# Two transformer blocks on one core: decay rows in one tile, decay chains in steps, another order of the projections

## Chip, cores and metric
One core of a Trainium2 chip. The metric is the device time of one execution in microseconds (us), the median of several.

## What is computed
The reference runs two blocks over 512 tokens of width 1024, in float32. Block 1: a gated feed-forward part (inner width 2816), a mixer, a second feed-forward part. Block 2: a mixer, then a feed-forward part with a convolution. What the change touches lies in the mixers.

In the first mixer a state-space branch with 32 heads (four groups of eight) works in chunks of 128 tokens:

```python
dt = softplus(dt_raw + dt_bias)
a = (dt * a_head)                       # 32 heads x 512 tokens
a_cum = cumsum(a, within chunks)
Lmat = exp(where(causal, a_cum[l] - a_cum[s], -inf))
y_diag = (C B^T * Lmat) X
states = scan over chunks of B^T (exp(a_last - a_cum) X)
y_off = C prev * exp(a_cum)
```

Beside it runs a differential attention with 8 heads; both are gated and merged. In the second mixer a gated delta rule (8 heads in four pairs, chunks of 64 tokens) needs a similar decay row per head, `-exp(a_log) * softplus(..)`, summed up within chunks, and a row `beta` per head. Beside it an indexer scores all keys for each query, keeps the 128 highest, and a sparse attention uses only these.

## The kernel before
Everything is held transposed: features on the 128 partitions, the 512 tokens as columns. A projection (`ugemm`) makes a 128 x 512 tile from eight 128 x 128 blocks of a weight panel. Each float32 operand is split into a high part, rounded to fp32r, and the low rest; a block is three fp32r matmuls, high x high, high x low and low x high (L1679 to L1681), 24 a projection. A panel of 512 KB is loaded by SyncE, its high part is copied out by ScalarE (L2020) and its low part made by VectorE (L2321).

The order of all work is written by a planner when the kernel is built. It keeps an estimated clock for each engine, advanced by a table of costs, and draws steps from a main stream (the projections, in the order of the strings ORDER1 and ORDER2) and side streams (the recurrent parts, the attention, the indexer). A side step is issued once what it needs is due on TensorE's clock (`ready`), provided that VectorE's and ScalarE's clocks are at most AHEAD = 6.0 us in front of TensorE's. If no side can go, the main stream takes a quarter of a projection. Every engine then runs its own queue in the planned order, with semaphores. Tiles of 128 x 512 for intermediate values are pages of a pool (`fp`); `room(n)` holds the main stream until n pages are free.

In the order strings, of the first mixer: t is the projection of dt, z, g the projections of a group (z four, g six), b the branch output of a group (eight), a and c a head's q, k and v, E and F gates, r a wait for pages. Of the second: n the narrow panel with decay and beta, p a pair's six projections, x the indexer's inputs (all made ahead at the stage's start), z a pair's gates, h a hold until the pair's preparation (`gdn_prep`) is done, d a query head, k keys and values.

The parts that the change touches:

- `decay` (VectorE L2478 to L2490, ScalarE L2125 to L2129): one step that holds the softplus (L2456 to L2475), in which VectorE and ScalarE answer each other three times, the scan (L2486), the high part of the sums (L2129, rows 0 to 31 of page 16 of `mR`) and the low part (L2489, page 17).
- `ssd_front` (L1762 to L1768): for each of the 32 heads, the head's row of sums is spread over 128 partitions by two matmuls with a column of a 32-row identity as weights, one on the high and one on the low rows. `ssd_from` (L1770 to L1778) does so for two heads at once with `selR`, 16 times, and goes on with three 128 x 128 products (L1778). `ssd_y` (L1781 to L1787) multiplies 128 x 64 weights.
- `narrow` (VectorE L2651 to L2674): bias, sigmoid on ScalarE, copy (L2661), the same softplus over 128 rows, the scan, in one step. `gdn_decay` (L1839) and `gdn_att` (L1846) spread the decay and the beta row of two heads with 32-row weights of 64 columns; L1853 is the product behind L1846.
- `ix_score` and `ix_top` (L2839 to L2862): scores of the indexer, then 15 rounds for each of three query blocks; a round takes out the eight highest (L2859) and finds the next eight (L2862).
- L2760 closes a level of the delta rule's triangular solve, and L1913 is the first product that uses its result.

Of the kernel before, what the change touches and what calls it, by code (L numbers as in the profile page):

```python
# [13 lines left out]
L = 512  # L14
# [31 lines left out]
def _layout():  # L46
    at = 0
    for name, n in (
# [14 lines left out]
         "neg": (128, 128), "incl64": (256, 64), "id64": (320, 64), "level": (384, 384), "reset64": (768, 512)}  # L63
NCA, NCB = 1280, 1280
# [58 lines left out]
def costs(s):  # L123
# [23 lines left out]
    if k == "ix_top":  # L147
        return [("DVE", 0.3 + 0.27 * w, "dve_idx.top")]
# [6 lines left out]
    if k == "gdn_fold" and s["lev"] == 5:  # L155
# [20 lines left out]
    "decay": [("DVE", 0.7), ("ACT Exp", 0.63), ("DVE", 0.42), ("ACT Ln", 0.63), ("DVE", 0.7), ("ACT Exp", 0.63), ("DVE", 2.7), ("ACT Exp", 0.2),  # L176
              ("DVE", 1.7, "dve_ssd.scan"), ("ACT", 0.62), ("DVE", 0.69, "dve_ssd.aclo")],
# [6 lines left out]
    "ssd_front": [("PE", 0.59), ("DVE", 0.69, "dve_ssd.seg"), ("DVE", 0.43), ("ACT Exp", 0.65, "act_ssd.E")],  # L184
# [3 lines left out]
    "ssd_from": [("PE", 1.6, "pe_ssd.off"), ("ACT Exp", 0.65, "act_ssd.EA"), ("DVE", 0.56, "dve_ssd.EA"), ("DVE", 0.56, "dve_ssd.off")],  # L188
    "ssd_y": [("PE", 1.03, "pe_ssd.y"), ("DVE", 0.69, "dve_ssd.y")],
    "turn_v": [("PE", 0.45, "pe_att.turn_v"), ("ACT", 0.6, "act_att.V")],  # L190
    "narrow": [("DVE", 0.9), ("ACT Sigmoid", 0.63), ("DVE", 1.1), ("ACT Exp", 0.63), ("DVE", 0.42), ("ACT Ln", 0.63), ("DVE", 0.7),
               ("ACT Exp", 0.63),
               ("DVE", 5.0, "dve_gdn.nar")],
# [31 lines left out]
def build(nc, d, out):  # L225
# [29 lines left out]
    with ExitStack() as ph:  # L255
        con[0] = sb(ph, "con1", [128, NCA])
        mR[0] = sb(ph, "mR1", [128, 18, L], R)
        idR = sb(ph, "idR", [128, 32], R)
        selR = sb(ph, "selR", [32, 4, 128], R)
        fB[0] = sb(ph, "fB1", [128, NB1, L])  # L260
# [134 lines left out]
    def ready(*xs, banks=0):  # L395
        def now():
# [3 lines left out]
            return t <= clock["PE"] and max(clock["DVE"], clock["ACT"]) <= clock["PE"] + AHEAD  # L400
# [401 lines left out]

    def decay_side():
# [3 lines left out]
        e1.release(("dve_soft.s5", s))  # L807
        w.release(("dve_soft.s4", s))
        ln.release(("dve_soft.s6", s))
        a.release(("dve_ssd.scan", s))  # L810
# [2290 lines left out]
```

## Time and profile before

| | us |
|---|---|
| median of 3 runs | 2619.51 (2619.28 to 2620.69) |
| the profiled execution | 2619.71 |
| its span, first to last instruction | 2617.9 |
| TensorE busy | 2534.8 (97%), 13762 matmuls |
| weight loads (PEld) busy | 2013.2 (77%) |
| VectorE busy | 1549.4 (59%) |
| ScalarE busy | 1060.3 (41%) |
| mean granted clock | 0.992 of 2.4 GHz |

The stages in the span: first feed-forward part to 370 us, state-space part of the first mixer from 402 to about 800, attention to about 1068, merge and output to 1185, second feed-forward part to 1555, second mixer from 1584 to 2201, the rest is the last feed-forward part. Rows of a timeline give start, duration, engine, line, operation, tiles, and in brackets the idle time before and what ended it. PEld is the weight load, PE the matmul; "issue" is a wait for nothing that the profile shows. Matmuls overlap, so the distance of their starts counts, not their durations.

### The profile page before, as it was taken

How to read it: one execution, taken by the hardware profiler on the slowest of the kernel's cores; microseconds unless marked ns; L12 is line 12 of the kernel's file. 1: busy time of each engine (PE TensorE's matmuls, PEld its weight loads, DVE VectorE, ACT ScalarE, POOL GpSimd, SP SyncE). 2: the span in 40 equal slices, each digit the busy share in tenths (PEclk: the TensorE clock that was granted, in tenths of full speed). 3: DMA queues.
4: the chain of work that ended last, by engine and by line, in shares of the span. 5: the costliest groups of instructions: out<-in, count | busy, mean ns of one | idle time of the engine just before them, and what ended most of it. 6: DMA issues, size and time to landing. Idle time of an engine off the chain costs nothing. (4 is left out here: it accounts for less than half of the span.)

```text
span 2617.9 us, 33764 instructions
## 1 busy us (share of the span) xinstructions
PE 2534.8 (97%) x13762; PEld 2013.2 (77%) x13762; DVE 1549.4 (59%) x2438; ACT 1060.3 (41%) x1654; POOL 3.6 (0%) x12
## 2 busy tenths in 40 slices
PE   7999999999999999999999999989999999999998
PEld 6888877777777777787888877767777687888886
DVE  5444248686766755356444237678866566677733
ACT  4223234555344545544222335443434254444421
POOL 0000000000000000000000000000000000000000
PEclk9999999999999999999999999999999999999999
DMA  4333332222221212222333332202111112233332
GB/s 143 97 97 95 100 97 77 68 73 73 65 73 63 75 65 73 89 97 80 97 97 95 95 103 73 81 25 69 54 50 34 57 57 65 95 98 98 95 95 77
DMA packets 59194, 209.94 MB, mean 80 GB/s; under 512 B 6560, under 2 KB 6560, under 8 KB 59040
## 3 DMA queue, kind: packets, MB, share of 16 engines
q1 hardware_dynamic: 57600, 204.38, 24.6%
q10 hardware_dynamic: 1440, 3.41, 0.4%
q8 instruction: 109, 1.79, 0.3%
q14 instruction: 45, 0.37, 0.0%
HBM read 205.66 MB, written 2.10 MB: 79 GB/s over the span
## 5 line engine op out<-in xcount | busy, mean ns | idle before, releaser
L1679 PE MATMUL bank<-uR,hl 128*128 128x512 f32 x2160 | 875.5, 405 | 25.4 <-DVE uR L2333 11.9
L1681 PE MATMUL bank<-uR,hl 128*128 128x512 f32 x2160 | 845.4, 391 | 0.0
L1680 PE MATMUL bank<-uR,hl 128*128 128x512 f32 x2160 | 844.9, 391 | 0.0
L2321 DVE TENSOR_TENSOR hl<-raw,hl 128x1024 fp32r<-128x1024 f32 (+1 forms) x391 | 471.9, 1208 | 577.4 <-ACT hl L2020 576.3
L1679 PEld LDWEIGHTS bank<-uR,hl 128*128 128x128 f32 x2160 | 407.7, 189 | 143.4 <-issue 39.7
L2020 ACT CAST hl<-raw 128x1024 fp32r<-128x1024 f32 (+1 forms) x391 | 401.8, 1030 | 249.7 <-PE bank L1681 238.8
L1681 PEld LDWEIGHTS bank<-uR,hl 128*128 128x128 f32 x2160 | 407.3, 189 | 87.4
L1680 PEld LDWEIGHTS bank<-uR,hl 128*128 128x128 f32 x2160 | 408.1, 189 | 85.5 <-issue 6.5
L1679 PE MATMUL bank<-act,hl 128*128 128x512 f32 x528 | 206.6, 391 | 0.0
L1681 PE MATMUL bank<-act,hl 128*128 128x512 f32 x528 | 205.4, 389 | 0.0
L1680 PE MATMUL bank<-act,hl 128*128 128x512 f32 x528 | 205.4, 389 | 0.0
L2326 DVE TENSOR_TENSOR fA<-bank,fA 128x512 f32<-128x512 f32 x132 | 90.8, 690 | 135.5 <-PE bank L1681 135.5
L2003 ACT ACTIVATE fA<-fA 128x512 f32<-128x512 f32 (+1 forms) x123 | 76.6, 629 | 206.3 <-DVE fA L2326 123.4
L2087 ACT CAST act<-fA 128x512 fp32r<-128x512 f32 x66 | 41.0, 621 | 283.6 <-DVE fA L2416 193.5
L1679 PE MATMUL bank<-mR,hl 128*128 128x512 f32 x320 | 127.4, 398 | 0.1
L1681 PE MATMUL bank<-mR,hl 128*128 128x512 f32 x320 | 124.7, 390 | 0.0
L1680 PE MATMUL bank<-mR,hl 128*128 128x512 f32 x320 | 124.6, 389 | 0.0
L1680 PEld LDWEIGHTS bank<-act,hl 128*128 128x128 f32 x528 | 99.1, 188 | 21.3 <-issue 0.7
L1679 PEld LDWEIGHTS bank<-act,hl 128*128 128x128 f32 x528 | 99.1, 188 | 21.1 <-issue 0.7
L1681 PEld LDWEIGHTS bank<-act,hl 128*128 128x128 f32 x528 | 99.1, 188 | 20.6
L2001 ACT ACT_TABLE_LOAD x52 | 66.7, 1283 | 67.3 <-PE bank L1681 17.9
L2003 ACT ACTIVATE fB<-fB 128x512 f32<-128x512 f32 (+1 forms) x105 | 63.7, 628 | 61.4 <-DVE fB L2539 49.0
(463 smaller groups left out, 2610.3 us busy)
## 6 DMA issues: line engine op xcount, KB each, us to landing
raw<-in_win SPq DMA_DIRECT2D x147, 512.0 KB, 3.5
raw<-in_w SPq DMA_DIRECT2D x44, 512.0 KB, 3.5
raw<-in_w1g SPq DMA_DIRECT2D x22, 512.0 KB, 3.5
raw<-in_w1u SPq DMA_DIRECT2D x22, 512.0 KB, 3.5
raw<-in_w2g SPq DMA_DIRECT2D x22, 512.0 KB, 3.5
raw<-in_w2u SPq DMA_DIRECT2D x22, 512.0 KB, 3.5
raw<-in_w1d SPq DMA_DIRECT2D x16, 512.0 KB, 3.5
raw<-in_wssd SPq DMA_DIRECT2D x16, 512.0 KB, 3.5
```

The source lines that it names most:

```text
L1679: e.matmul(s.bank[:, :], h[:, 0, w], hi, start=s.first and q == 0, stop=False)
L1680: e.matmul(s.bank[:, :], h[:, 0, w], lo, start=False, stop=False)
L1681: i = e.matmul(s.bank[:, :], h[:, 1, w], hi, start=False, stop=s.last and q == n - 1)
L2001: e.preload_act_table_set(sets[0])
L2003: return e.activation(o, i, func, **k)
L2020: e.copy(hl[j % NHL][:, 0, 0:s.width], raw[j % NRAW][:, 0:s.width]).then_inc(*sig("act_split.hi", s))
L2087: e.copy(s.a[:, 0, s.j, :], s.p[:, :]).then_inc(*sig("act_ffn.hi", s))
L2321: e.tensor_tensor(h[:, 1, 0:s.width], x[:, 0:s.width], h[:, 0, 0:s.width].bitcast(F), ALU.subtract).then_inc(*sig("dve_split.lo", s))
L2326: e.tensor_tensor(s.x[:, :], s.b[:, :], s.r[:, :], ALU.mult).then_inc(*sig("dve_norm.scaled", s))
```

## The change
The two 32-row parts of the decay sums go to rows 0 to 31 and 32 to 63 of one page, the rest of its 128 rows is zero, and the weights (`idR`, `selR`) come from a constant that has the 32-row identity twice and zeros below. So one matmul over 128 rows stands for two over 32. The delta rule's two spreads use all 128 rows of `nar`, with columns of the 128-row identity. The softplus becomes three steps (`soft_a`, `soft_b`, `soft_c`), the rest of `decay` two (`decay`, `decay_lo`), that of `narrow` one (`narrow_scan`), each issued once its predecessor is due. The indexer's steps are issued only with the other engines' clocks at most BEHIND = 2.0 us in front of TensorE's, and a round's cost goes from 0.3 to 0.45 us plus 0.27 for each 128 columns. The orders change, and the projections of the groups, z, pairs, gates and plain tiles wait for six free pages.

```diff
+BEHIND = 2.0
+ROOM, ROOM2 = 6, 6
-ORDER1 = "t z0 g0 z1 g1 r12 g2 z2 b0 a0 g3 b1 a1 b2 z3 a2 a3 c4 c5 b3 c6 c7 E F"
-ORDER2 = "n p0 p1 x z0 h0 z1 p2 r10 z2 p3 d0 z3 r12 k r10 d1"
+ORDER1 = "t g0 g1 z0 z1 g2 b0 z2 b1 g3 a0 a1 b2 z3 a2 a3 c4 b3 c5 c6 c7 E F"
+ORDER2 = "n p0 x p1 p2 z0 h0 z1 p3 z2 d0 d1 z3 k"
...
-        return [("DVE", 0.3 + 0.27 * w, "dve_idx.top")]
+        return [("DVE", 0.45 + 0.27 * w, "dve_idx.top")]
...
-    "ssd_front": [("PE", 0.59), ...
+    "ssd_front": [("PE", 0.23), ...
-    "ssd_from": [("PE", 1.6, "pe_ssd.off"), ...
+    "ssd_from": [("PE", 1.3, "pe_ssd.off"), ...
...
-    def ready(*xs, banks=0):
+    def ready(*xs, banks=0, ahead=AHEAD):
...
-            return t <= clock["PE"] and max(clock["DVE"], clock["ACT"]) <= clock["PE"] + AHEAD
+            return t <= clock["PE"] and max(clock["DVE"], clock["ACT"]) <= clock["PE"] + ahead
...
+    def softplus(x, xt, rows):
+        e1, w, ln = fp.take(), fp.take(), fp.take()
+        a = step("soft_a", x=x, xt=xt, e1=e1, rows=rows)
+        yield from ready(("act_soft.e", a))
+        b = step("soft_b", e1=e1, w=w, ln=ln, a=a, rows=rows)
+        yield from ready(("act_soft.inv", b))
+        c = step("soft_c", x=x, e1=e1, w=w, ln=ln, b=b, rows=rows)
...
+        return c
...
     def decay_side():
         dt = S1["dt"]
-        e1, w, ln, a, ac = fp.take(), fp.take(), fp.take(), fp.take(), fp.take()
-        s = step("decay", dt=dt, e1=e1, w=w, ln=ln, a=a, ac=ac, after=t_phase)
+        a, ac = fp.take(), fp.take()
+        c = yield from softplus(dt, list(dt.t), slice(0, 32))
+        yield from ready(("dve_soft.s6", c))
+        s = step("decay", dt=dt, a=a, ac=ac, c=c, after=t_phase)
         a.release(("dve_ssd.scan", s))
+        yield from ready(("act_ssd.achi", s))
+        s3 = step("decay_lo", ac=ac, s=s)
...
         for i in range(4):
+            yield from room(ROOM)
             b = yield from ugemm(WIN[16 + 4 * g + i])
...
         for h2 in range(4):
-            yield from ready(x, iq[h2], banks=2)
+            yield from ready(x, iq[h2], banks=2, ahead=BEHIND)
...
-            yield from ready(sc)
+            yield from ready(sc, ahead=BEHIND)
             step("ix_top", i=i, n=n, W=W, sc=sc, wk=wk)
...
-            one = idR[0:32, s.H:s.H + 1].broadcast_to([32, 128])
-            e.matmul(s.b[:, :], one, mR[0][0:32, 16, :], start=True, stop=False)
-            e.matmul(s.b[:, :], one, mR[0][0:32, 17, :], start=False, stop=True).then_inc(*sig("pe_ssd.cum", s))
+            one = idR[:, s.H:s.H + 1].broadcast_to([128, 128])
+            e.matmul(s.b[:, :], one, mR[0][:, 16, :], start=True, stop=True).then_inc(*sig("pe_ssd.cum", s))
...
-            e.matmul(s.b[:, :], selR[:, s.i, :], mR[0][0:32, 16, :], start=True, stop=False)
-            e.matmul(s.b[:, :], selR[:, s.i, :], mR[0][0:32, 17, :], start=False, stop=True).then_inc(*sig("pe_ssd.ea", s))
+            e.matmul(s.b[:, :], selR[:, s.i, :], mR[0][:, 16, :], start=True, stop=True).then_inc(*sig("pe_ssd.ea", s))
...
-                t = e.matmul(s.b[r, :], con[1][0:32, h:h + 1].broadcast_to([32, 64]), s.nar[0:32, :], start=True, stop=True)
+                t = e.matmul(s.b[r, :], con[1][:, h:h + 1].broadcast_to([128, 64]), s.nar[:, :], start=True, stop=True)
...
-                t = e.matmul(s.bb[r, :], con[1][32:64, h:h + 1].broadcast_to([32, 64]), s.nar[32:64, :], start=True, stop=True)
+                t = e.matmul(s.bb[r, :], con[1][:, h:h + 1].broadcast_to([128, 64]), s.nar[:, :], start=True, stop=True)
...
-            e.tensor_copy(idR[:, :], con[0][:, 0:32]).then_inc(*sig("dve_ssd.idR", s))
+            e.tensor_scalar(mR[0][64:128, 16, :], con[0][64:128, 0:L], 0.0, None, ALU.mult)
+            e.tensor_copy(idR[:, :], cc(0, "stack")).then_inc(*sig("dve_ssd.idR", s))
...
-            e.tensor_tensor(mR[0][0:32, 17, :], s.ac[0:32, :], mR[0][0:32, 16, :].bitcast(F),
+            e.tensor_tensor(mR[0][32:64, 16, :], s.ac[0:32, :], mR[0][0:32, 16, :].bitcast(F),
...
+    put(a, "stack", (p < 64) & (p % 32 == f[:, :32]))
```

## Rows read from the trace of the kernel before

**Rows 1.** The page, part 1: busy us, share of the span, instructions
```profile
PE 2534.8 (97%) x13762; PEld 2013.2 (77%) x13762; DVE 1549.4 (59%) x2438; ACT 1060.3 (41%) x1654; POOL 3.6 (0%) x12
```

**Rows 2.** Busy time by stretches: from:to, length, then each engine's
```profile
402.40:450.00 47.60, 42.63 (x182) 34.26 (x183) 37.93 (x61) 22.46 (x34) 0.00 (x0) 0.93 0.28 89
450.00:800.00 350.00, 347.77 (x1726) 265.11 (x1726) 254.32 (x376) 167.82 (x246) 1.81 (x3) 1.00 0.22 71
...
1700.00:1760.00 60.00, 51.17 (x616) 38.33 (x617) 45.13 (x108) 28.66 (x47) 0.00 (x0) 0.94 0.09 29
```

**Rows 3.** TensorE's waits: line <- releaser: total us, times, longest
```profile
PE bank L1679 <- DVE hl L2321: 8.4, 4, 4.9
PE bank L1913 <- DVE gx L2760: 6.7, 1, 6.7
PE bank L1679 <- DVE fA L2449: 5.1, 1, 5.1
...
PE bank L1959 <- DVE fA L2809: 2.9, 1, 2.9
...
PE bank L1931 <- DVE fA L2787: 2.1, 1, 2.1
```

**Rows 4.** Timeline of TensorE around one L1767 and L1768
```profile
469.14 0.39 PE L1680 MATMUL bank<-uR,hl 128*128 128x512 f32 x1
469.14 0.19 PEld L1681 LDWEIGHTS bank<-uR,hl 128*128 128x128 f32 x1
469.37 0.39 PE L1681 MATMUL bank<-uR,hl 128*128 128x512 f32 x1
469.68 0.18 PEld L1767 LDWEIGHTS bank<-mR,idR 32*128 32x128 f32 x1 [0.36 <-issue]
...
470.02 0.39 PE L1768 MATMUL bank<-mR,idR 32*128 32x512 f32 x1
...
470.68 0.39 PE L1680 MATMUL bank<-uR,hl 128*128 128x512 f32 x1
```

**Rows 5.** L1767 alone (min/median/max ns), and groups: busy us, mean ns | idle
```profile
L1767 PE MATMUL bank<-mR,idR x32: 382/495/497, 469.7 to 781.1; 32*128 32x512 f32 x32
...
L1767 PE MATMUL bank<-mR,idR 32*128 32x512 f32 x32 | 14.9, 467 | 0.0
...
L1773 PE MATMUL bank<-mR,selR 32*128 32x512 f32 x16 | 7.9, 492 | 0.0
...
L1774 PE MATMUL bank<-mR,selR 32*128 32x512 f32 x16 | 6.1, 382 | 0.0
```

**Rows 6.** Timeline of TensorE: L1787 then L1773; the load of L1853 behind L1846
```profile
493.20 1.09 PE L1787 MATMUL bank<-fB 128*64 128x128 f32 x16
494.22 0.18 PEld L1773 LDWEIGHTS bank<-mR,selR 32*128 32x128 f32 x1 [0.17 <-issue]
...
1672.29 0.25 PEld L1853 LDWEIGHTS bank<-gx 128*64 128x64 f32 x5 [0.81 <-issue]
```

**Rows 7.** Timeline: the weight split behind the decay chain, and TensorE's next matmul
```profile
434.53 1.23 DVE L2321 TENSOR_TENSOR hl<-raw,hl 128x1024 fp32r<-128x1024 f32 x1 [0.34 <-ACT hl L2020]
...
435.81 0.79 PE L1679 MATMUL bank<-uR,hl 128*128 128x512 f32 x1 [4.88 <-DVE hl L2321]
```

**Rows 8.** Stretches at half clock: length, TensorE busy (x), granted clock, DMA share, GB/s
```profile
434.40:441.20 6.80, 5.39 (x13) 0.50 0.25 77
...
1622.20:1625.60 3.40, 2.92 (x7) 0.50 0.46 143
1738.30:1745.10 6.80, 4.76 (x44) 0.50 0.01 2
```

**Rows 9.** Timeline of VectorE: the wait for the sigmoid in the narrow chain
```profile
1610.08 0.43 DVE L2661 COPY fB<-fB 128x512 f32<-128x512 f32 x1 [2.89 <-ACT fB L2003]
```

**Rows 10.** Timeline of VectorE: the starts of two search rounds of 256 columns
```profile
1733.80 0.09 DVE L2859 MATCH_VALUE_LOAD fB<-small,fB 128x8 f32 x1
...
1734.78 0.09 DVE L2859 MATCH_VALUE_LOAD fB<-small,fB 128x8 f32 x1
```

More of the change, by code:

```diff
@@ L825, in project_group @@
             yield
+        yield from room(ROOM)
         b = yield from ugemm(WIN[32 + g])
@@ L828, in project_group @@
         yield
+        yield from room(ROOM)
         b = yield from ugemm(WIN[36 + g])
@@ L946, in project_z @@
             here = id(WIN[4 * g + i]) in ahead
+            yield from room(0 if here else ROOM)
             b = yield from ugemm(WIN[4 * g + i])
@@ L1221, in narrow_side @@
         b = S2["narrow"]
-        nar, w, e1, w1, ln, g_ = fp.take(), fp.take(), fp.take(), fp.take(), fp.take(), fp.take()
-        s = step("narrow", b=b, nar=nar, w=w, e1=e1, w1=w1, ln=ln, g=g_)
-        b.release(("dve_gdn.bias", s))
-        e1.release(("dve_soft.s5", s))
-        w1.release(("dve_soft.s4", s))
-        ln.release(("dve_soft.s6", s))
+        nar, w, g_ = fp.take(), fp.take(), fp.take()
+        s0 = step("narrow", b=b, nar=nar, w=w)
+        b.release(("dve_gdn.bias", s0))
+        c = yield from softplus(w, [("dve_gdn.copy", s0)], slice(0, 128))
+        yield from ready(("dve_soft.s6", c))
+        s = step("narrow_scan", nar=nar, w=w, g=g_, c=c, s=s0)
         w.release(("dve_gdn.scan", s))
-        nar.t = [("dve_gdn.nar", s), ("act_gdn.beta", s)]
+        nar.t = [("dve_gdn.nar", s), ("act_gdn.beta", s0)]
         g_.release(("dve_gdn.nar", s))
@@ L1247, in project_gdn @@
         for name, j in (("q", h), ("k", 8 + h)):
+            yield from room(ROOM2)
             b = yield from ugemm(W2[j])
@@ L1257, in project_zg @@
     def project_zg(h):
-        yield from room(6)
+        yield from room(ROOM2)
         b = yield from ugemm(W2[24 + h])
@@ L1420, in plain @@
             return ahead.pop(id(W2[j]))
+        yield from room(ROOM2)
         b = yield from ugemm(W2[j])
@@ L2455, in dt_in, with soft_a, soft_b @@
                             ALU.add).then_inc(*sig("dve_ssd.dt", s))
-        def softplus(s, x, e1, w, ln, rows):
-            after(*e1.after)
-            e.scalar_tensor_tensor(out=e1[rows, :], in0=x[rows, :], scalar=-1.0, in1=x[rows, :], op0=ALU.mult,
+        def soft_a(s):
+            r = s.rows
+            after(*s.xt, *s.e1.after)
+            e.scalar_tensor_tensor(out=s.e1[r, :], in0=s.x[r, :], scalar=-1.0, in1=s.x[r, :], op0=ALU.mult,
                                    op1=ALU.max).then_inc(*sig("dve_soft.s0", s))
-            go.wait_ge(*on("act_soft.e", s))
-            after(*w.after)
-            e.tensor_scalar(w[rows, :], e1[rows, :], 1.0, None, ALU.add).then_inc(*sig("dve_soft.s1", s))
+        def soft_b(s):
+            r = s.rows
+            go.wait_ge(*on("act_soft.e", s.a))
+            after(*s.w.after)
+            e.tensor_scalar(s.w[r, :], s.e1[r, :], 1.0, None, ALU.add).then_inc(*sig("dve_soft.s1", s))
@@ L2474, in softplus @@
                                    op1=ALU.add).then_inc(*sig("dve_soft.s6", s))
[L2475 removed]
         def decay(s):
[L2478 to L2479 removed]
+            go.wait_ge(*on("dve_soft.s6", s.c))
             go.wait_ge(*on("act_ssd.aex", s))
@@ L2661, in narrow, with narrow_scan @@
             e.tensor_copy(w[:, :], nar[:, :]).then_inc(*sig("dve_gdn.copy", s))
-            go.wait_ge(*on("dve_gdn.copy", s))
-            softplus(s, w, s.e1, s.w1, s.ln, every)
+        def narrow_scan(s):
+            nar, w, g = s.nar, s.w, s.g
+            go.wait_ge(*on("dve_soft.s6", s.c))
             go.wait_ge(*on("act_gdn.gex", s))
```

79 lines of the change are left out of this document (41 added, 38 removed).

## Prediction
> **What bounds the kernel now.** The page comes first: TensorE is busy for 97% of the span and VectorE for 59% [rows 1]. A busy TensorE can still be slow, so two further things are read: where it stands still, and how far apart its matmuls start. By stretches, the change lies in the two mixing stages, and there losses are to be seen. From 402 to 450 us it is busy 42.6 of 47.6 us, and from 1700 to 1760 us 51.2 of 60 [rows 2]. The list of waits names them. The longest single waits inside the mixers are 4.9 us for a weight split on VectorE (L2321), 5.1 us for a convolution tap (L2449), 6.7 us for L2760 of the delta rule and 2.9 us for L2809 [rows 3]. TensorE's own work is thus nearly the whole time, and a microsecond off it is a microsecond off the end wherever the other engines keep up.
>
> **Part 1: the decay rows in one tile.** The reader should look at starts, not at durations, because matmuls overlap. In the main product L1680 and L1681 start 0.23 us apart, and the weight load of L1681 is issued with the matmul before it [rows 4]. In front of L1767, which uses 32 rows of the array, this stops: its load comes 0.31 us behind the start of L1681, and the same is seen behind L1768. From the start of L1681 to that of L1680 behind the pair 1.31 us pass with four matmuls in them (L1681, L1767, L1768, L1679). Four at 0.23 are 0.92, so going to another tile shape and back costs 0.39, or 0.2 each way.
> The change turns two 32-row products into one over 128 rows. 48 matmuls go (one L1768 behind each of the 32 L1767, and 16 L1774 [rows 5]): 48 x 0.23 = 11.0 us. How many changes of shape go? L1767 takes 382 ns at least and 495 in its median; the longer ones began with their own load still under way. Its mean is 467 [rows 5], so (467 - 382)/(495 - 382) of the 32, some 24, follow a change, and with a mean of 492 all 16 of L1773 do. That is 40 blocks. Some 12 of the L1773 stand right behind L1787, whose products are 64 columns wide [rows 6] (head pairs two to four of each of four groups, where ssd_y is directly followed by ssd_from), so their way in stays; one way out leads into L1787 too. What goes is 28 ways in and 39 ways out, 67 x 0.2 = 13.4 us. Part 1 gives 24.4 us. Bounds: 11.0 if the changes of shape stay for some reason, 27.0 if all 80 go.
> What full-height tiles do is in the same rows: the load of L1681 is issued with the start of L1680. The Trainium skill, page "TensorE: Matmul & The Clock Gate", section Part 3, has it that a weight load overlaps matmuls in flight only where its row group differs, so that a full-height load would never be hidden; by that rule part 1 would be worth some 16 us (rival B), and the rows disagree with it. The skill's page "TensorEngine Tiling (Array Packing)", Key Properties, has a change of tiling mode drain the array; by that rule part 1 is worth the 24.4, and the rows agree (0.2 us each way).
> The delta rule's two broadcasts (L1839, L1846) also go to 128 rows, but stay 64 columns wide. They still differ from the main product on both sides; only L1846 now has the shape of L1853 behind it, whose load is issued only when the array has emptied, 0.81 us after the load before it [rows 6]: 4 x 0.2 = 0.8 us.
> Additions: one VectorE operation of 64 rows and 512 columns at the start of the mixer (the copy of that width in L2661 takes 0.43 us [rows 9]), beside TensorE work that doesn't wait for it; 16 KB more constants; 128 for 32 rows in four small GpSimd copies, for which no L1773 waits (its idle time is 0.0 [rows 5]). Priced at nothing, at most 0.5 us together if the VectorE queue has no slack there.
>
> **Part 2: the decay chains in steps.** Before, VectorE goes through the softplus chain and the scan with ScalarE's answers between, and the weight split queued behind is taken only at 434.53, after the last operation of the chain (L2489). TensorE has run out of weights by then and stands 4.88 us, until 435.81 [rows 7]. It then runs at 1.2 GHz (granted clock 0.50 to 441.2): 13 matmuls in 5.39 us [rows 8], which at 0.23 each would take 3.0, so 2.4 us more. Together 7.3. With the chain issued in pieces, each only once the one before is due, the split and the taps go between the pieces; the chain has work for nobody until group 0 is projected, six panels of 5.5 us (24 x 0.23) later. The same in the second mixer: VectorE sits 2.89 us in front of L2661, waiting for ScalarE's sigmoid, and goes on with the chain [rows 9]; TensorE waits 5.1 us [rows 3] and then runs 7 matmuls at 1.2 GHz in 2.92 us [rows 8] for 1.6, 1.3 us more. Together 6.4. The wait for the sigmoid stays inside its step, but the ten operations of the chain behind it no longer stand before the split. I take both whole: 13.7 us; at the least nothing, if what ScalarE does between the pieces (other tables to load, for one) makes a split late all the same.
>
> **Part 3: the search nearer, and earlier.** The 45 rounds of the indexer are queued by a plan that counts a 256-wide round at 0.3 + 2 x 0.27 = 0.84 us. Rounds start 0.98 apart [rows 10]. The plan lets VectorE be 6 us ahead, and the true lead is longer. So rounds stand in the queue before L2760, and L1913 waits 6.7 us for it [rows 3], as long as seven rounds; behind that, 4.8 us of TensorE's work run at 1.2 GHz [rows 8], half of it lost, 2.4 us. The new costs (0.99, and 2 us of lead) cut that to about two rounds; and the new order puts pair 2's six projections ahead of the hold for pair 0, at which TensorE has only side work today. I take 9.1 us. The wait of 2.1 us for L2787 and that for L2809 (a normalisation, not a search) I leave in.
>
> **Part 4: order and room.** Nothing is computed more or less. What it can bring is at most what waits remain in the mixers, about 10 us; what it can cost are holds: the main stream now stops before most projections when fewer than six pages are free, and its copies, splits and 24 matmuls stop with it. No row shows such a hold; the nearest is the TensorE wait of 5.1 us for a tap [rows 3]. I book one, 5 us of loss, also for the hand-offs that become shorter of cover as TensorE gets faster in the first mixer (347.8 of 350 us busy today, VectorE 254 [rows 2]).
>
> **The sum**: 24.4 + 0.8 + 13.7 + 9.1 - 5 = 43.0 us. The profiled execution took 2619.71 us (span 2617.9 and 1.8 around it), 0.2 above the median of 2619.51. 2619.7 - 43.0 = 2576.7.
>
> **Rivals.**
> A. The matmuls go, the stalls only move. Two streams are re-planned, and a stall taken out in one place may return in another: part 1 and the chains pay less than they say. For it: each mixer has many short waits now (L1931 is one [rows 3]). Against: the three big ones each have a cause that the edit removes. Gain: the 25.2 of part 1, and of the 22.8 of parts 2 and 3 between 8 less and 8 more than is lost in new stalls: 2587 to 2603, say 2595. Chance 0.2.
> B. The change of shape isn't what holds the loads back: L1767's weights are one column repeated, and it may be they, or the pair's one bank, that cost. Then only the 48 matmuls and the part of their loads that shows, 495 less 382, go: 48 x (0.23 + 0.11) = 16 us in place of 24.4, or 11 with nothing of the loads: 2576.7 + 8 to 13 = 2585 to 2590. Against it: L1773, with ordinary weights, waits as L1767 does, and L1787 and L1853 show the same [rows 6]. Chance 0.07.
> C. More comes than I say: no hold, the earlier search also frees L2809 and the 2.1 us wait, 5 + 2.9 + 2.1 on top: 2566.7, or with the changes of shape at L1787 2564. Chance 0.08.
> D. Slower than before: the room rule. Every hold in which side work can't fill in costs what the 6.7 us wait costs with its half clock, 9.1. It must eat 48.0 us, so it decides from six such holds on; eight would give 2619.7 - 48.0 + 73 = 2645. For it: 60-odd projections now ask. Against: TensorE has side work nearly always in both mixers (3 of 350 us idle). Chance 0.03.
> E. The forecast, 2576.7, its own range 2566 to 2590: chance 0.62.
> A measurement of this kernel can tell some 0.2%, 5 us, from no change. Faster by more: all of A, B, C and E but for a tail, 0.94. Within it: 0.03. Slower: 0.03. The range from 2562 to 2604 holds E, B, A and most of C.
>
> **What would show it.** In the trace of after: L1767 and L1773 once each, near 382 ns where a full-size product precedes, their load issued with the matmul before; no gap of 3 us or more near 431 and 1617, nor the half clock behind them; no long row of search rounds before an L2760; the state-space stage, 450 to 800 us now, shorter by some 24 us. Part 1 is wrong if the loads of L1767 still come 0.3 us late; part 2 if L2321 or L2449 still holds L1679 there for microseconds; part 3 if L1913 waits for L2760; part 4 if there are new gaps in front of L1679 whose releaser is a page's last reader.

## The result, and the profile after

The changed kernel takes 2601.87 us (median of 6 runs, 2600.93 to 2603.68), the kernel before, on the same chip, 2620.54. The ratio is 0.9927 with an interval of 0.9914 to 0.994: 18.7 us, or 0.7%, less. The forecast was 43.0 us less. "Half clock" below is a granted clock of 0.50, 1.2 of 2.4 GHz. The profiled execution took 2600.94 us, span 2599.1.

Part 1 of the page of the changed kernel, against [rows 1]:

```profile
PE 2516.7 (97%) x13714; PEld 2011.8 (77%) x13714; DVE 1547.8 (60%) x2439; ACT 1060.0 (41%) x1654; POOL 3.7 (0%) x12
```

48 matmuls are gone and TensorE is busy for 18.1 us less, which is nearly the whole gain. The gaps between its matmuls add up to 61.7 us before and 61.1 after: as much standing still as ever, although three large waits were taken away. They changed places: in the first mixer the gaps grew from 20.3 to 28.0 us, from the second mixer on they shrank from 32.2 to 23.0. What half clock takes (half of TensorE's busy time in such stretches) is 14.0 us before and 17.2 after. The same stretches as in [rows 2]:

```profile
402.40:450.00 47.60, 46.44 (x203) 37.74 (x202) 40.97 (x61) 20.19 (x30) 0.00 (x0) 1.00 0.31 100
450.00:800.00 350.00, 336.27 (x1719) 268.02 (x1717) 264.88 (x416) 173.72 (x270) 2.09 (x3) 0.99 0.22 71
1700.00:1760.00 60.00, 60.00 (x675) 43.74 (x673) 36.74 (x61) 30.66 (x52) 0.00 (x0) 1.00 0.17 53
```

The first and the last row are where parts 2 and 3 were to act: TensorE 42.6 to 46.4 of 47.6 us, and 51.2 to 60.0 of 60. The middle one shows where time was lost: in the state-space part TensorE is now busy for 336.3 of 350 us, before for 347.8. TensorE's waits name the place (the lines of L1679 to L1681 are now L1704 to L1706, L1787 is L1810, L2321 is L2347; L2576 applies the mask to a head's decay matrix):

```profile
PE bank L1810 <- DVE fB L2576: 6.5, 3, 3.5
PE bank L1829 <- ACT fB L2223: 6.2, 8, 1.3
PE bank L1810 <- DVE fA L2576: 6.0, 2, 3.9
PE bank L1704 <- DVE hl L2347: 3.5, 3, 1.2
```

The split waits 3.5 us in all where it was 8.4 [rows 3], and the waits for a tap of L2449 and for L2760 are gone. In their place TensorE waits 12.5 us for the mask. One of these places in TensorE's timeline:

```profile
591.47 0.40 PE L1706 MATMUL bank<-mR,hl 128*128 128x512 f32 x1
591.79 1.09 PE L1810 MATMUL bank<-fB 128*64 128x128 f32 x16
592.82 0.51 PE L1797 MATMUL bank<-mR,selR 128*128 128x512 f32 x1
593.16 0.83 PE L1801 MATMUL bank<-fB,fA 128*128 128x128 f32 x6
593.74 0.71 PE L1792 MATMUL bank<-mR,idR 128*128 128x512 f32 x2
596.59 0.29 PE L1810 MATMUL bank<-fB 128*64 128x128 f32 x1 [2.13 <-DVE fA L2576]
...
602.25 1.20 PE L1810 MATMUL bank<-fB 128*64 128x128 f32 x16 [3.47 <-DVE fB L2576]
603.38 0.80 PE L1704 MATMUL bank<-uR,hl 128*128 128x512 f32 x1
```

Between 591.5 and 603.4 us no projection product (L1704 to L1706) starts. TensorE has only the heads' own chain (spread, subtract, exponential, mask, product), and each link waits for the one before. Behind it L1704 takes 0.80 us, since from 603.1 to 606.5 us the granted clock is 0.50. Three such stretches of more than 6 us stand in the first mixer (27.3 us in all, of which 12.3 are gaps); before there was none.

Part 1 itself looks as it should. TensorE and its loads around an L1792 (L1767 before), against [rows 4]:

```profile
473.74 0.40 PE L1706 MATMUL bank<-uR,hl 128*128 128x512 f32 x1
...
473.98 0.39 PE L1792 MATMUL bank<-mR,idR 128*128 128x512 f32 x1
474.21 0.40 PE L1704 MATMUL bank<-uR,hl 128*128 128x512 f32 x1
```
```profile
473.75 0.19 PEld L1792 LDWEIGHTS bank<-mR,idR 128*128 128x128 f32 x1
473.98 0.19 PEld L1704 LDWEIGHTS bank<-uR,hl 128*128 128x128 f32 x1
```
```profile
L1792 PE MATMUL bank<-mR,idR x32: 388/396/481, 474.0 to 756.3; 128*128 128x512 f32 x32
L1797 PE MATMUL bank<-mR,selR x16: 390/500/796, 489.3 to 763.3; 128*128 128x512 f32 x16
```

The load of L1792 is issued with the matmul before it, starts are 0.23 us apart on both sides, and the median is 396 ns where it was 495 [rows 5]. L1797 keeps its 500 ns: behind L1810, with weights of 64 columns, the cost of the way in stays, as the prediction had it.

### The profile page after: what moved, and what is told of

It reads as the page before. It is cut to its first block, busy times and chain, and to the rows that moved or that the text cites. A ratio compares the mean times of both kernels' runs of the same rounds, so it can differ in the third digit from the quotient of the medians.

```text
span 2599.1 us, 33677 instructions
## 1 busy us (share of the span) xinstructions
PE 2516.7 (97%) x13714; PEld 2011.8 (77%) x13714; DVE 1547.8 (60%) x2439; ACT 1060.0 (41%) x1654; POOL 3.7 (0%) x12
## 4 chain that ended last, share of the span: by engine, by line
PE 86%; DVE 8%; ACT 4%; issue 1%; DMA 0%; DVEq 0%; SPq 0%; ACTq 0%
PE bank L1704 25%; PE bank L1706 24%; PE bank L1705 24%; PE bank L1904 2%; PE bank L1743 1%; DVE hl L2347 1%; ACT fB L2026 1%; DVE small L2658 1%; ACT hl L2043 1%; PE bank L1829 1%; ACT fA L2026 1%; DVE fB L2654 1%; PE bank L1719 1%; PE bank L1721 1%; PE bank L1724 1%
## 5 line engine op out<-in xcount | busy, mean ns | idle before, releaser
L1704 PE MATMUL bank<-uR,hl 128*128 128x512 f32 x2160 | 873.6, 404 | 15.6 <-DVE uR L2359 11.9
L1706 PE MATMUL bank<-uR,hl 128*128 128x512 f32 x2160 | 844.9, 391 | 0.0
L2347 DVE TENSOR_TENSOR hl<-raw,hl 128x1024 fp32r<-128x1024 f32 (+1 forms) x391 | 471.8, 1208 | 585.1 <-ACT hl L2043 584.2
L1704 PEld LDWEIGHTS bank<-uR,hl 128*128 128x128 f32 x2160 | 407.6, 189 | 126.2 <-issue 27.2
L1706 PEld LDWEIGHTS bank<-uR,hl 128*128 128x128 f32 x2160 | 407.2, 188 | 87.7
L1704 PE MATMUL bank<-act,hl 128*128 128x512 f32 x528 | 206.6, 391 | 0.0
L1706 PE MATMUL bank<-act,hl 128*128 128x512 f32 x528 | 205.5, 389 | 0.0
L1704 PE MATMUL bank<-mR,hl 128*128 128x512 f32 x320 | 128.0, 400 | 1.0 <-DVE fB L2616 1.0
L1706 PE MATMUL bank<-mR,hl 128*128 128x512 f32 x320 | 125.9, 394 | 0.0
L1705 PEld LDWEIGHTS bank<-act,hl 128*128 128x128 f32 x528 | 99.1, 188 | 21.3 <-issue 0.7
L1704 PEld LDWEIGHTS bank<-act,hl 128*128 128x128 f32 x528 | 99.1, 188 | 21.1 <-issue 0.7
L1706 PEld LDWEIGHTS bank<-act,hl 128*128 128x128 f32 x528 | 99.1, 188 | 20.7
L2026 ACT ACTIVATE fB<-fB 128x512 f32<-128x512 f32 x105 | 63.9, 628 | 58.0 <-DVE fB L2572 34.3
L2026 ACT ACTIVATE fB<-fB,small 128x512 f32<-128x512 f32 (+3 forms) x73 | 41.5, 569 | 111.9 <-DVE small L2660 75.5
```

The source lines that it names most:

```text
L1704: e.matmul(s.bank[:, :], h[:, 0, w], hi, start=s.first and q == 0, stop=False)
L1705: e.matmul(s.bank[:, :], h[:, 0, w], lo, start=False, stop=False)
L1706: i = e.matmul(s.bank[:, :], h[:, 1, w], hi, start=False, stop=s.last and q == n - 1)
L2026: return e.activation(o, i, func, **k)
L2347: e.tensor_tensor(h[:, 1, 0:s.width], x[:, 0:s.width], h[:, 0, 0:s.width].bitcast(F), ALU.subtract).then_inc(*sig("dve_split.lo", s))
```

## The experiments

For a comparison by stage, the traces are cut at the 3.7 us wait of the first matmul of each feed-forward or mixing part. "First mixer" is from that wait at 379 us to that at 1190 (times of before), "second and rest" from 1561 to the final wait of 1.44 us. The stage lengths come from the one profiled execution of each kernel. The second feed-forward part, with the same work in all of them, is 369.5 to 371.4 us there, because half clock falls differently; a difference of 1 to 2 us in a stage is therefore weak evidence. A median of another kernel belongs to its own comparison; before had 2620.5 to 2621.5 in all of them.

| kernel | median us | ratio to before | first mixer | second and rest |
|---|---|---|---|---|
| before | 2620.5 | 1 | 810.9 | 1045.1 |
| after | 2601.9 | 0.9927 | 802.4 | 1034.1 |
| rows_only | 2610.8 | 0.9956 | 799.3 | 1045.3 |
| order_only | 2639.8 | 1.0067 | 822.5 | 1053.6 |
| rows_undone | 2617.0 | 0.9977 | 819.5 | 1031.9 |
| first_as_before | 2598.2 | 0.9907 | 799.7 | 1032.9 |
| rows_pad | 2606.2 | 0.9935 | 795.9 | 1046.8 |
| after_pad | 2598.3 | 0.9906 | 800.9 | 1034.2 |
| room_only | 2642.2 | 1.0074 | 821.1 | 1055.1 |
| no_search | 2625.3 | 1.0013 | 803.8 | 1058.6 |
| one_step | 2622.9 | 1.0009 | 814.7 | 1045.5 |
| first_as_before_pad | 2594.0 | 0.9898 | 795.7 | 1033.8 |
| first_room_off | 2596.2 | 0.9907 | 798.2 | 1034.4 |
| second_room_off | 2617.4 | 0.9985 | 799.7 | 1052.1 |
| room_eight | 2611.0 | 0.9963 | 812.4 | 1034.2 |
| best | 2593.5 | 0.9897 | 796.0 | 1033.0 |
| turn_later | 2592.9 | 0.9888 | 793.6 | 1032.7 |

**rows_only: part 1 alone, on the plan of before.**

```diff
-            one = idR[0:32, s.H:s.H + 1].broadcast_to([32, 128])
-            e.matmul(s.b[:, :], one, mR[0][0:32, 16, :], start=True, stop=False)
-            e.matmul(s.b[:, :], one, mR[0][0:32, 17, :], start=False, stop=True)
+            one = idR[:, s.H:s.H + 1].broadcast_to([128, 128])
+            e.matmul(s.b[:, :], one, mR[0][:, 16, :], start=True, stop=True)
```

> The kernel before with part 1 alone: stacked decay rows, one product over 128 rows, the delta rule's two spreads over 128 rows. Chains, search, orders and room are before's, the planner's costs too, so the order of all steps is before's to the last one. Theory 1 (each part pays what it was sized at; the loss is made in the first mixer by the new order with its room for six pages): 24 to 25 us less than before, 2595 to 2597, TensorE's idle time in the first mixer near before's 20.3 us. Theory 2 (a faster TensorE uncovers VectorE and ScalarE there under any order): the first mixer's idle time rises to about 28 us as in the changed kernel, and only 13 to 17 us come off, 2603 to 2607.

It takes 2610.8 us, ratio 0.9956 (0.9941 to 0.997): 10.6 us less. That lies outside both ranges. Theory 2 was nearer, though not for its reason alone. Measured from each matmul's start to the next in the first mixer, gaps left out, L1767 and L1768 take 19.4 us before and 8.0 now, the spreads of ssd_from (L1773, L1774) 10.4 and 5.0, and L1778 behind them 12.3 and 9.4. That is 19.7. The long distances, about 0.31 to 0.35 us, between a full-size product and its neighbour are 97 instead of 144 and hold 4.7 us less beyond 0.2285 each. Together 24.4 us, what part 1 was sized at. A count without such a choice agrees within a microsecond: all distances of the first mixer together, gaps left out, are 17.5 us less, and against that stand 2.2 us more of half clock and about 4 of slower products (rows_pad, below), which puts part 1 itself at some 23.7. The time shows 10.6 because three things come on top. TensorE's waits of rows_only:

```profile
PE bank L1679 <- DVE hl L2320: 9.3, 4, 5.4
PE bank L1911 <- DVE gx L2759: 6.3, 1, 6.3
PE bank L1785 <- DVE fB L2542: 5.4, 3, 4.7
```

A wait of 4.7 us for the mask stands at 526.9 us, where before had none over 0.7; with a split 0.6 us longer the gaps in the first mixer are 5.9 us more. Behind the new wait are 6.8 us at half clock, in which TensorE is busy for 5.1, so some 2.5 are lost. The third is the place of a tile, and is taken up with rows_pad.

**order_only: part 4 alone (both strings and the rule), on the kernel before.**

```diff
-ORDER2 = "n p0 p1 x z0 h0 z1 p2 r10 z2 p3 d0 z3 r12 k r10 d1"
+ORDER2 = "n p0 x p1 p2 z0 h0 z1 p3 z2 d0 d1 z3 k"
+ROOM, ROOM2 = 6, 6
...
+            yield from room(ROOM)
```

> The kernel before with the new order strings and the room for six pages alone. Theory 1: slower than before. The first mixer of the changed kernel fell short of the sum by some 18 us, and in it TensorE waited 12.5 us for the decay mask of a head (L1810 for L2576), with three stretches at half clock of 3.4 us each; most of that should be here too, against which the second mixer's order brings a few: 2625 to 2636. Theory 2: the order is neutral, 2617 to 2623.

2639.8 us, ratio 1.0067 (1.0052 to 1.0082): slower by 18.4 us, more than theory 1 had. 11.6 of it are in the first mixer, 8.5 in the second.

**room_only: the rule without the strings.** Both strings are those of before, the `room(...)` calls and `ROOM, ROOM2 = 6, 6` stay.

> The kernel before with the rule of six free pages alone, both order strings as before. The new strings with the rule cost 18.4 us (order_only). Theory R (the rule costs: each hold of the main stream leaves TensorE with nothing but the chain it waits for): most of it is here, 2632 to 2642. Rival S (the strings cost, which put a group's projections closer to each other; the rule is needed for them and cheap): 2621 to 2626.

2642.2 us, ratio 1.0074 (1.0057 to 1.009), 20.7 us slower. All of the loss is the rule's, and the strings give some 2 us back by the medians, in no one stage. It costs 10.2 us in the first mixer and 10.0 behind. A stretch of room_only in each mixer, and the same place of the first mixer in before, from 653 to 672 us (second fence):

```profile
665.00:684.00 19.00, 14.47 (x81) 9.90 (x80) 13.61 (x25) 6.47 (x11) 0.60 (x1) 0.66 0.00 0
1835.00:1860.00 25.00, 14.94 (x196) 11.53 (x196) 24.00 (x54) 2.11 (x3) 0.00 (x0) 0.66 0.01 2
```
```profile
653.00:672.00 19.00, 19.00 (x106) 13.84 (x104) 12.60 (x21) 6.00 (x10) 0.00 (x0) 1.00 0.11 35
```

A hold is easy to see in such a row: no DMA at all, since no panel is used up, TensorE busy for 14.5 of 19 us, and a granted clock of 0.66 in the mean (1.00 up to 671.1 us, 0.50 from there). Before, the 19 us were full, with 106 matmuls instead of 81. The loss of the stretch is 4.5 us idle and 14.5 x 0.34 = 4.9 of clock, together 9.4. From 1835 to 1860 us the same shows in the second mixer, with VectorE busy for 24.0 of 25 us. From one projection product to the next, these two stretches are 21.3 us (from 664.7 us on, 10.6 lost) and 42.8 us (from 1813.1 on, 16.4 lost). In the first mixer of before none is longer than 6 us, and in the second its 7.1, 12.5 and 20.0 us from 1820 us on lose 0.2 together. Over the whole trace the gaps grow from 61.7 to 75.6 us, and what half clock takes (half of the busy time in those stretches) from 14.0 to 25.8.

**rows_undone: the changed kernel with two products over 32 rows.** The diff of rows_only, backwards; plan and costs stay.

> The changed kernel with two products over 32 rows again, its plan and its costs kept. Theory 1: part 1 adds up with the rest unless a stall covers it; the waits for the mask stand where TensorE has nothing else queued, and the 1.3 us of a pair are partly inside them: 18 to 24 us slower than the changed kernel, 2620 to 2626. Theory 2: part 1 was mostly eaten by the other engines: 8 to 14 us slower, 2610 to 2616.

2617.0 us, ratio 0.9977 (0.9967 to 0.9986). Part 1 is worth 15.2 us in the changed kernel by the medians, 13 by the two ratios. In the first mixer it gives 17.1, and behind it the changed kernel is 2.2 slower: from the second mixer on half clock takes 7.4 us there and 3.4 in rows_undone, while the gaps are alike (23.0 and 23.5). The time lies between the two theories. Against order_only it shows parts 2 and 3 together: 2639.8 - 2617.0 = 22.8 us, 21.7 of them in the second mixer.

**first_as_before: the first mixer in the order of before, with stacked rows.**

```diff
-ROOM, ROOM2 = 6, 6
+ROOM, ROOM2 = 0, 6
...
+        x = step("soft_a", x=dt, xt=list(dt.t), e1=e1, rows=slice(0, 32), nocost=True)
+        x = step("soft_b", e1=e1, w=w, ln=ln, a=x, rows=slice(0, 32), nocost=True)
+        c = step("soft_c", x=dt, e1=e1, w=w, ln=ln, b=x, rows=slice(0, 32), nocost=True)
         a, ac = fp.take(), fp.take()
...
         s = step("decay", dt=dt, a=a, ac=ac, c=c, after=t_phase)
```

> The first mixer in before's order to the last step (old ORDER1, no room rule, softplus and scan issued together, before's costs) but with the stacked rows; the second mixer as in the changed kernel. Theory 1: before less 24 us of part 1 less the 11 us that the second mixer gained: 2583 to 2588, faster than both kernels. The 4.9 us wait for the weight split at 431 us and its half clock are back. Theory 2: the first mixer is no better than in the changed kernel, and the wait for the chain is back on top: 2602 to 2608.

(ORDER1 is that of before, and the costs too.) 2598.2 us, ratio 0.9907 (0.9892 to 0.9922). It beats the changed kernel by 3.6 us, not by the 14 to 19 of theory 1; neither theory holds. Its first mixer is that of rows_only (799.7 and 799.3), its second that of the changed kernel (1032.9): stages add up. So the new order, with its rule and the split chain, costs the first mixer 2.7 us net. With the chain in one step it would be 15.0 (one_step, below: 814.7 against 799.7).

**rows_pad and after_pad: 128 unused bytes ahead of mR1.** The constants with the stacked identity are 32 columns longer, so mR1 starts 128 bytes later.

```diff
         con[0] = sb(ph, "con1", [128, NCA])
+        pad1 = sb(ph, "pad1", [128, 32])
         mR[0] = sb(ph, "mR1", [128, 17, L], R)
```

> Part 1 alone (as in rows_only) with an unused tile of 128 bytes between con1 and mR1, so that mR1 starts 256 bytes instead of 128 behind where it started before. Nothing else moves in the order. In rows_only the full-size products whose columns come from mR start 232.6 ns apart between 1100 and 1180 us, before 226.8; those that read uR are the same in both. Theory P (the place of mR1 in SBUF costs it): back to 227 ns, some 700 products in the first mixer by 5 to 6 ns, 4 us less than rows_only: 2606 to 2608. Rival Q (128 more bytes of anything, or the merged product, cause it): 232 ns stays, 2610 to 2611.

> The changed kernel with the same unused 128 bytes ahead of mR1. Theory P: its mR products go from 232.7 to 227 ns, 700 of them, 3.5 to 4.5 us less: 2597 to 2599. Rival Q: no difference, 2601 to 2603.

2606.2 and 2598.3 us: 4.6 and 3.6 us less, each in its own comparison with before. Theory P holds. 27 neighbouring products of the output projection in rows_only, first and last:

```profile
1099.77 0.40 PE L1681 MATMUL bank<-mR,hl 128*128 128x512 f32 x1
...
1105.83 0.40 PE L1680 MATMUL bank<-mR,hl 128*128 128x512 f32 x1
```

and 28 in rows_pad:

```profile
1099.73 0.39 PE L1682 MATMUL bank<-mR,hl 128*128 128x512 f32 x1
...
1105.85 0.39 PE L1682 MATMUL bank<-mR,hl 128*128 128x512 f32 x1
```

6.06 us over 26 distances are 233.1 ns, 6.12 over 27 are 226.7. From 1100 to 1170 us TensorE is full in both, but rows_only gets 303 matmuls through and rows_pad 308:

```profile
1100.00:1170.00 70.00, 70.00 (x303) 56.55 (x302) 34.48 (x42) 27.92 (x39) 0.00 (x0) 1.00 0.28 92
```
```profile
1100.00:1170.00 70.00, 69.91 (x308) 57.44 (x307) 34.51 (x43) 29.30 (x42) 0.00 (x0) 1.00 0.30 98
```

Busy time and durations hardly tell it (0.40 or 0.39 us), only the starts do. Products that read uR are as far apart in both kernels, 228 ns in the mean. The tiles behind mR1 moved with it, but only products that read mR became slower.

**no_search: the changed kernel without part 3.**

```diff
-        return [("DVE", 0.45 + 0.27 * w, "dve_idx.top")]
+        return [("DVE", 0.3 + 0.27 * w, "dve_idx.top")]
-            yield from ready(sc, ahead=BEHIND)
+            yield from ready(sc)
```

> The changed kernel without part 3: a round of the search at the old cost, six microseconds of lead. Theory 1 (part 3 pays what it was sized at, 9.1 us, in this order too): 2609 to 2612, with L1904 waiting for microseconds for the last operation of a solve's level. Theory 2 (the new order alone takes the search away from the solve): 2602 to 2604. Parts 2 and 3 together gave 22.8 us (rows_undone against order_only), as sized; if part 3 is worth more than 9.1, part 2 is worth less.

2625.3 us, ratio 1.0013 (1.0003 to 1.0022): 23.4 us slower than the changed kernel, more than twice the 9.1 and outside both ranges. The waits are not at L1904 but at other links of the delta rule's chain:

```profile
PE bank L1952 <- DVE fB L2816: 8.8, 4, 6.5
...
PE bank L1980 <- DVE fB L2841: 4.7, 1, 4.7
PE bank L1741 <- DVE fB L2819: 3.4, 1, 3.4
```

VectorE in front of that L2816, the state of the recurrence (four rounds of 512 columns, 1.51 us each, come before L2783, and one more behind it):

```profile
1827.97 0.09 DVE L2891 MATCH_VALUE_LOAD fB<-small,fB 128x8 f32 x1
...
1833.31 0.70 DVE L2894 MAX8 small<-fB 128x8 f32<-128x512 f32 x1
1834.04 0.69 DVE L2783 TENSOR_TENSOR gx<-gx,con 128x512 f32<-128x512 f32 x1
...
1836.16 0.61 DVE L2816 SCALAR_TENSOR_TENSOR fB<-fB,small,bank 128x128 f32<-128x128 f32 x2
```

**one_step: the changed kernel without part 2.** Each chain is one step again.

> The changed kernel without part 2: the two decay chains each in one step again, all else kept. Part 2 was sized at 13.7 us (7.3 in the first mixer, 6.4 in the second). Theory 1 (it pays as sized): 2613 to 2617, with the 4.9 us wait for the split near 431 us and the 5.1 us wait for a tap near 1615 back, each with half clock behind it. Theory 2 (the chain's end comes later when it is issued in pieces, and the first heads wait for it, so that it pays less): 2603 to 2609; parts 2 and 3 together gave 22.8 us, and part 3 alone is worth 23.4 in the changed kernel.

2622.9 us, ratio 1.0009 (1.0 to 1.0019): 21.0 us slower, 12.3 in the first mixer and 11.4 behind. The expected waits are back:

```profile
PE bank L1795 <- DVE fB L2552: 9.1, 3, 3.9
PE bank L1689 <- DVE hl L2330: 8.9, 4, 5.4
...
PE bank L1689 <- DVE fA L2458: 5.1, 1, 5.1
```

Theory 1 was nearer, and also too low. It is 23.4 for part 3 and 21.0 for part 2, but 22.8 for both. In the second mixer, counted from order_only (1053.6), part 3 without part 2 gives 8.1 us (one_step, 1045.5), part 2 without part 3 gives nothing (no_search, 1058.6), and both give about 20 (1031.9 to 1034.1).

**first_as_before_pad.** The pad in first_as_before.

> first_as_before (first mixer in before's order with the stacked rows, second as changed: 2598.2 us) with mR1 moved by 128 bytes. The two gains add: 4.6 us less, as between rows_only and rows_pad: 2593 to 2595. If the first mixer's stalls took the gain of the shorter products: 2596 to 2598.

2594.0 us, ratio 0.9898 (0.9883 to 0.9912), as expected.

**first_room_off and second_room_off: the rule off in one mixer of after_pad.**

```diff
-ROOM, ROOM2 = 6, 6
+ROOM, ROOM2 = 0, 6
```

(second_room_off has `6, 0` and nothing else; first_room_off also the two costs of before.)

> after_pad (2598.3 us) with the rule of six pages off in the first mixer; for a plan that keeps its pages the costs of ssd_front and ssd_from are before's again (0.59 and 1.6 us). Holds planned in the first mixer: two of together 15 us, in place of five of together 22 us. Theory R (the rule's holds make the waits for the mask L2576): the first mixer is 6 to 10 us shorter, 2588 to 2593. Rival (any plan of the shortened heads waits there, the chain from L1792 to L1810 being the bound): 2597 to 2601.

> after_pad with the rule off in the second mixer alone. On the kernel before the rule cost 10 us there (room_only). Theory R1 (it costs the same in any plan): 2588 to 2592. Theory R2 (with the search held to 2 us of lead the second mixer is bound by its chains, and the rule costs nothing more or helps): 2597 to 2606.

2596.2 us and 2617.4 us. In the first mixer 2.7 us come off, less than theory R had and near its rival: the five waits for the mask became two of the products C B (L1777, for L2541), together 12.5 us as well. In the second mixer, where the rule had cost 10 us on the kernel before, taking it away now costs 17.9 (1034.2 to 1052.1), more than either theory had. But this edit takes away more than the change had put in: the kernel before held each z of the second mixer for six pages and had r10, r12 and r10 in ORDER2, and with ROOM2 = 0 and the new string all of these are gone; only the holds of the later query heads and gates stay. The 17.9 us are the price of less holding than the kernel before had, not the worth of the rule against it. Of second_room_off:

```profile
PE bank L1705 <- DVE hl L2348: 10.7, 4, 7.2
PE bank L1983 <- DVE fA L2844: 10.2, 1, 10.2
PE bank L1824 <- DVE fB L2947: 7.5, 4, 6.0
```

TensorE stands 10.2 us up to 2050 us, while VectorE works through rounds of the search and then the last operations of the recurrence (L2844); 7.2 up to 2072 and 6.0 up to 2182 follow. The likely reading is that without these holds the projections run ahead and are used up, so that nothing is left to cover the recurrence and the search. Which of the holds prevents it was not tested.

**room_eight: more of the rule in the first mixer.** `ROOM, ROOM2 = 8, 6` in after_pad.

> after_pad (2598.3 us) with eight pages instead of six wanted in the first mixer. The main stream is planned to be held seven times for 32.8 us in place of five times for 22.0. Theory R (a hold shows on the chip as a wait of TensorE for the mask L2576, with half clock behind it): 8 to 14 us slower, 2606 to 2612, the waits for L2576 up from 12.5 us to 20 or more. Rival (the planned holds are filled by side work and the waits come from the heads' chain itself): 2597 to 2601.

2611.0 us, ratio 0.9963 (0.995 to 0.9975). 10.8 us more of planned hold gave 11.5 us more of first mixer (800.9 to 812.4), and the waits for the mask (L2577 there) rose to 21.2:

```profile
PE bank L1811 <- DVE fA L2577: 14.5, 4, 5.3
...
PE bank L1811 <- DVE fB L2577: 6.7, 2, 3.5
```

Theory R holds here as to what a hold costs, about its planned length. In first_room_off it did not: 7 us less of planned hold gave 2.7.

**best and turn_later: the chain in pieces, on the plan of before.** best is first_as_before_pad with each piece two quarters of a projection behind the last; turn_later also puts decay_turn later.

```diff
+        x = step("soft_a", x=dt, xt=list(dt.t), e1=e1, rows=slice(0, 32), whole=True)
+        t = clock["PE"]
+        while clock["PE"] < t + 2.0:
+            yield HOLD
+        x = step("soft_b", e1=e1, w=w, ln=ln, a=x, rows=slice(0, 32), nocost=True)
...
+        t = clock["PE"]
+        while clock["PE"] < t + 20.0:
+            yield HOLD
         yield from ready(("dve_ssd.scan", s), banks=1)
```

> first_as_before_pad (2594.0 us) with the first mixer's decay chain in five pieces after all, each piece put two quarters of a projection behind the one before it; every other step of both mixers keeps its place. The chain's own loss, as sized before the change, is the wait for the split (5.4 us here, near 432 us) and the half clock behind it (6.8 us long, 2.4 us lost). Theory 1 (part 2 pays as sized when nothing else moves): 7 to 8 us less, 2586 to 2587.5. Theory 2 (another wait takes its place, on the conv taps or later at the first heads, since the sums come some 8 us later): 2590 to 2594.

> best (2593.5 us) with decay_turn, the transposes of the scanned sums on TensorE, put five quarters of a projection later, so that TensorE doesn't meet it before the scan is done (441.9 us in best, where it came to it at 436.4). Theory 1 (the wait was only displaced, and goes once nothing of the chain stands early in TensorE's queue): 5.6 us of wait and some 3 us of half clock go, 2585 to 2587. Theory 2 (VectorE has no slack for the chain before the first group, and the wait moves to a split, a tap or the first heads): 2590 to 2594.

2593.5 us and 2592.9 us: the expected 7 us did not come in either. TensorE in best (L1777 is the first transpose of decay_turn), and the waits of turn_later:

```profile
436.02 0.39 PE L1731 MATMUL bank<-uR,hl 128*128 128x512 f32 x1
441.98 0.63 PE L1777 MATMUL bank<-con,fA 32*128 32x32 f32 x4 [5.58 <-DVE fA L2542]
```
```profile
PE bank L1838 <- DVE fB L2604: 6.4, 3, 5.7
PE bank L1732 <- DVE fA L2503: 4.2, 2, 4.0
```

The wait for the split (5.4 us) became one for the scan (5.6), and with that step moved one for a tap (4.0) and 0.9 more for the mask. The scan is late in best because of what ScalarE does between the pieces of the chain:

```profile
428.57 1.28 ACT L2049 ACT_TABLE_LOAD   x1
429.87 2.19 ACT L2051 ACTIVATE fB<-fB 128x512 f32<-128x512 f32 x4
432.08 1.28 ACT L2049 ACT_TABLE_LOAD   x1
433.37 1.35 ACT L2051 ACTIVATE fA<-fA 32x512 f32<-32x512 f32 x2
```
```profile
434.83 0.68 DVE L2527 TENSOR_TENSOR fB<-fB,fA 32x512 f32<-32x512 f32 x1 [3.91 <-ACT fA L2051]
```

ScalarE's function for the four tiles of z0 goes in between, with a table load on either side, and VectorE stands idle for 3.91 us until ScalarE comes back to the chain; turn_later has the same 3.91 us. In first_as_before_pad, where the chain is issued together, that wait is 0.78 us. In the changed kernel g0 and g1 stand before z0, and no table load falls between the chain's pieces; the first behind it is at 452.58 us. So the split chain gives its gain there only together with the new order of the first projections: with the order of before it gave nothing or 1 us (best, turn_later), and the new order without it lost 12.3 (one_step). The fastest of all are these two and first_as_before_pad, level within their intervals; turn_later is at 0.9888 (0.9871 to 0.9904), 28.5 us less than before in its own comparison and 9 less than the changed kernel.

## Why the prediction was wrong

The direction was right, and the wide range (2562 to 2604) held the time, but the forecast of 43.0 us was more than twice the 18.7, and its own range (2566 to 2590) did not hold it. What came is the number of rival A, "the matmuls go, the stalls only move", with 2587 to 2603 and a chance of 0.2, and as A says, the gaps together are as long as before. Its sum is not what ran, though: it leaves part 1 its 25.2 us.

Two terms failed. How the missing 24.3 us (23.4 by the medians of these runs) are shared between them depends on the order in which the parts are put in. With order and rule first (room_only, order_only, rows_undone, after), part 4 is 13.4 us short (18.4 lost where 5 were booked) and part 1 10.0 (15.2 where 25.2 were). With part 1 first (rows_only, first_as_before, after), part 1 is 14.6 short (10.6), the changes in the second mixer 2.9 (12.6 of 15.5), and chain, order and rule in the first mixer 5.9 (3.6 lost where 7.3 - 5 were to be gained). Part 1 falls short either way.

1. **Part 4**: "No row shows such a hold; the nearest is the TensorE wait of 5.1 us for a tap [rows 3]. I book one, 5 us of loss". The runs show 20.7 us for the rule alone and 18.4 with the new strings, on the kernel before. Two long stretches without a projection product came with it, one in each mixer. The first lost 10.6 us, near the 9.1 that rival D took for a hold with its half clock, the second 16.4. So one was booked where there were two, and at 5 us, a wait without the half clock behind it. The plan is made when the kernel is built, and the number and length of its holds can be had from it. The argument against, that TensorE is 3 us idle in 350, speaks of the time when projections fill every gap, and the rule takes away just these. In the changed kernel the rule is not shown to be a loss of that size: without it the first mixer gains 2.7 us, and the second, which then holds less than the kernel before did, loses 17.9.

2. **Part 1, 24.4 us.** As a sum of distances it was right (19.7 + 4.7), and rival B is out: L1792 still has one column repeated as its weights, and its median is 396 ns. The Trainium skill, page "TensorE: Matmul & The Clock Gate", section Part 3, says that a weight load overlaps matmuls in flight only where its row group differs; here too the trace disagrees (full-height load at 473.75, matmul before at 473.74). But the time shows 10.6 alone and 13 to 15 in the changed kernel. "Part 1 gives 24.4 us" was booked whole, though the text had said that a microsecond off TensorE counts only "wherever the other engines keep up", and for the state-space part this was never tested. On the same plan the shorter products alone brought a wait of 4.7 us for the mask: the slow products had been part of what hid that chain. Of the difference in rows_only, 5.9 us are gaps, 2.5 half clock and some 4 the place of mR1, which leaves about 12 of the 24.4; the first mixer shows 11.6. "16 KB more constants", in what was "Priced at nothing", was the wrong term there: they moved a tile.

3. **Parts 2 and 3, 13.7 and 9.1 us.** Their sum of 22.8 came out at 22.8 (rows_undone against order_only). It is largely luck: 21.7 lie in the second mixer, where 6.4 + 9.1 were booked, and 3.0 in the first, where 7.3 were, and singly they do not add up (23.4 and 21.0 in the full change). The named waits went as forecast [rows 3, 7, 9]. What was missed is that in the second mixer a backlog on VectorE of either kind shows up at the next link of the same chain, as the waits of no_search do. And what the prediction gave as the least that part 2 could bring, "at the least nothing, if what ScalarE does between the pieces (other tables to load, for one) makes a split late all the same", is what best shows.

4. **The delta rule's 0.8 us.** The distances behind its 32 products are 8.0 us before and 7.5 after, so about 0.5 came. It can't be seen in the time: the 2.2 us by which the changed kernel is longer than rows_undone from the second mixer on are less than the 4.0 more that half clock takes.

The terms as measured in the first of the two orders, each kernel against the one before it: rule +20.7, strings -2.3, parts 2 and 3 -22.8, part 1 -15.2. The sum is -19.6, against -18.7; the kernel before had a median of 2620.5 beside the changed kernel and of 2621.4 to 2621.5 beside the others.

What stays open: what the rule is worth in the second mixer once parts 2 and 3 are in, against the holds that the kernel before had; and whether a plan exists that keeps the first mixer's chain split, its order and no hold. Parts 2 and 3 were not run on the plan of before in the second mixer, where each was only taken out of the changed kernel.

## What to carry to other kernels

Where an order is planned, a removed stall is worth its length only if nothing else gets in its place: best and turn_later took the same 5 us away and got 1, since work with two table loads came between the pieces of the chain. Before booking a gain on the engine that is busy for 97%, ask which chain its slow instructions were hiding. Count the holds that a new rule makes, and price them with the half clock behind them; a stretch without any DMA and with a granted clock of 0.66 is how one looked here. When a constant's size changes, look at what lies behind it.

## What was not expected of the hardware

The place of a tile in SBUF changes the rate of full-size products that read their columns from it: 232.7 ns from start to start in the mean between 1100 and 1170 us with mR1 128 bytes further (rows_only), 227 ns with it 0 or 256 bytes further (before, rows_pad), at a granted clock of 1.00 in all three. With some 700 such products in the first mixer that is 4 us. What the products do otherwise, and the weights' tile, are the same. All 17 traces agree: the five with mR1 128 bytes further (after, rows_only, first_as_before, no_search, one_step) have 232.7 to 233.3 ns in this stretch, the twelve others 226.8 or 226.9. No other distances than these were tried, so what alignment counts is not known.
